# Output norm of a gated linear attention: one-column means, inverse roots on 16 columns, and transposes in place of wide products

## The reference, cut to what matters

```
o_g, s_new = gla(qg, kg, vg, la, s0)                       # (tokens, 4 heads, 256)
o_b = rmsnorm(o_g, g_gla_norm) * silu(gr)                  # mean over the 256 values of a head
merged = sigmoid(ga) * (o_a @ w_branch_a) + sigmoid(gb) * (o_b @ w_branch_b)
x = x + merged @ w_out                                     # then a mixture of 32 experts
```

## Time and profile before

| | |
|---|---|
| Median of 3 runs | 1103.74 us (1100.39 to 1105.07) |
| Span of the profiled execution | 1101.6 us; the profile gives no other time for it |
| PE busy | 1004.5 us (91% of the span) |
| DVE, ACT, POOL busy | 390.0, 281.0, 218.9 us |
| TensorE clock granted, mean of the span | 0.958 |
| Chain that ended last | PE 38%, transfers 26%, DVE 4% |

### The profile page before, as it was taken

The page is one execution under the profiler, slowest core; times in us unless marked ns, Lnnn a source line. Parts: engine busy times, 40 slices in busy tenths (PEclk is TensorE's granted clock), DMA queues, the critical chain, the costliest instruction groups (busy, mean ns, idle before and its releaser), DMA issues.

```text
span 1101.6 us, 15368 instructions
## 1 busy us (share of the span) xinstructions
PE 1004.5 (91%) x6369; PEld 696.1 (63%) x6369; DVE 390.0 (35%) x732; ACT 281.0 (26%) x456; POOL 218.9 (20%) x126
## 2 busy tenths in 40 slices
PE   8999999989999999999999899988787779877895
PEld 6996778869998799999997333333333433333232
DVE  7246333342786583322445211211101111111027
ACT  5435444455465452222215000000000000000012
POOL 0331121203221453443220011111001110011000
PEclk9999999999999999999999999988898899899898
DMA  9332512113211133343386999999999999999994
GB/s 232 79 90 77 180 41 58 39 39 96 58 41 49 48 97 86 116 130 96 124 364 245 373 424 427 425 425 426 429 427 427 428 426 429 429 426 425 423 412 152
DMA packets 108943, 267.57 MB, mean 243 GB/s; under 512 B 21821, under 2 KB 88797, under 8 KB 95666
## 3 DMA queue, kind: packets, MB, share of 16 engines
q1 hardware_dynamic: 104178, 258.06, 61.1%
q0 software_dynamic: 4704, 8.64, 2.1%
HBM read 256.12 MB, written 18.17 MB: 249 GB/s over the span
## 4 chain that ended last, share of the span: by engine, by line
PE 38%; DMA 26%; DVE 4%; issue 2%; ACT 1%; SPq 0%; DVEq 0%; POOLq 0%; ACTq 0%
DMA we<-in_w_exp_up 24%; PE proj L1062 18%; PE proj L1543 11%; PE proj L1559 3%; DMA zc<-expert_out 1%; PE bank L1389 1%; PE bank L1439 1%; DMA expert_out<-yo,sidx 1%; PE bank L1569 1%; PE proj L1345 1%; DVE x_rows L2637 1%; DVE xsT L2564 1%; ACT ex L1890 1%; PE proj L1545 0%; DVE x_rows L2644 0%
## 5 line engine op out<-in xcount | busy, mean ns | idle before, releaser
L1543 PE MATMUL proj<-we,xsT 128*64 128x512 f32 x512 | 249.1, 644 | 69.6 <-DMA we<-in_w_exp_up 61.5
L1545 PE MATMUL proj<-we,xsT 128*64 128x512 f32 x512 | 249.5, 644 | 0.0
L916 POOL TENSOR_TENSOR wlo<-raw,whi 128x1024 fp32r<-128x1024 f32 x68 | 156.2, 2298 | 382.1 <-PE proj L1062 358.9
L1543 PEld LDWEIGHTS proj<-we,xsT 128*64 128x64 f32 x512 | 73.2, 149 | 209.4 <-issue 193.4
L1062 PE MATMUL proj<-hT_hi,whi 128*128 128x272 f32 x688 | 146.4, 294 | 0.2 <-ACT grs L1824 0.2
L1062 PE MATMUL proj<-hT_hi,wlo 128*128 128x272 f32 x688 | 144.7, 292 | 0.0
L1062 PE MATMUL proj<-hT_lo,whi 128*128 128x272 f32 x688 | 144.5, 292 | 0.0
L2556 DVE TENSOR_TENSOR hg<-hg,proj 64x512 f32<-64x512 f32 x32 | 22.1, 690 | 309.1 <-ACT hg L2062 295.9
L2062 ACT ACTIVATE hg<-proj 64x512 f32<-64x512 f32 x30 | 17.7, 590 | 424.0 <-PE proj L1545 424.0
L1559 PE MATMUL proj<-we,hT 128*64 128x512 f32 x256 | 115.2, 592 | 2.0 <-DVE hT L2559 1.1
L1560 PE MATMUL proj<-we,hT 128*64 128x512 f32 x256 | 115.2, 593 | 0.0
(11 more groups left out here) (372 smaller groups left out, 1407.6 us busy)
## 6 DMA issues: line engine op xcount, KB each, us to landing
we<-in_w_exp_gate SPq DMA_DIRECT2D x31, 2048.0 KB, 32.1
we<-in_w_exp_up SPq DMA_DIRECT2D x31, 2048.0 KB, 36.5
we<-in_w_exp_down SPq DMA_DIRECT2D x31, 2048.0 KB, 38.8
raw<-in_w_in SPq DMA_DIRECT2D x43, 512.0 KB, 3.8
x_rows<-in_x_prompt SPq DMA_DIRECT2D x8, 512.0 KB, 4.8
raw<-in_w_branch_b SPq DMA_DIRECT2D x8, 512.0 KB, 3.9
raw<-in_w_out SPq DMA_DIRECT2D x8, 512.0 KB, 4.0
zc<-expert_out SPq DMA_DIRECT2D x4, 1024.0 KB, 17.6
```

Of the source, the lines that this page charges most:

```text
L916: nc.gpsimd.tensor_tensor(lo[:, 0:c], raw[n % NRAW][:, 0:c], hi[:, 0:c].bitcast(F32), ALU.subtract).then_inc(w_split, 1)
L1543: pe.matmul(proj[0:SLOTS, s, 0, :], xsT[:, k, cols], wg[:, k * FF:(k + 1) * FF], start=(k == 0), stop=(k == KD - 1))
L1545: mm = pe.matmul(proj[64:64 + SLOTS, s, 0, :], xsT[:, k, cols], wu[:, k * FF:(k + 1) * FF], start=(k == 0), stop=(k == KD - 1))
```

## The change

The means are no longer spread over 128 partitions by a wide product. DVE first adds the two squared tiles of a head (`sum_squares`). Then the squares are the stationary operand and one column of `mean256` moves through: each product gives the means of 128 tokens as one column, on the partitions of these tokens (`mean_columns`, two heads at a time, 16 products of one column for the four heads, each two matmul records). ACT takes the root of eight columns at once (`roots`), DVE inverts eight columns (`inverse_roots`), and PE turns each column back: it transposes the column, broadcast to 128x128, into a bank (`turn_roots`), so that the inverse roots stand on all 128 partitions. `normed_output` reads them there, in PSUM, instead of from SBUF. The decode tokens keep their wide form, with their bank changed.

PE's order changes too. `wa` 4 is issued in four parts, between which the decode outputs stand three, three and two, and the first turn of roots. The second one-column means stand behind `wa` 4. `ga` 5 is issued in eight parts, with the second turn of roots behind the second part and the decode means, head by head, behind parts 3 to 6.

```diff
@@ buffers
-    ors = [D_("ors0", [P, SEQ])]
...
-    ors.append(D_("ors1", [P, SEQ]))
+    o_root = D_("o_root", [P, 4 * GH])
@@ -722,6 +721,17 @@
     x_turned = bank[:, 0:2, :].rearrange("p a b -> p (a b)")[:, 0:TOK]
+    def root_col(h, i):
+        return 4 * h + i
+    def root_rows(h):
+        return bank[:, (1, 3)[h % 2], :]
+    COLUMNS_DONE, ROWS_DONE, DEC_DONE = (1, 4), (2, 3, 5, 6), 7
     def output_part(h):
         return (slice(None), slice(2 * h, 2 * h + 2), slice(0, SEQ)) if h < GH else (slice(None), slice(None), slice(SEQ, TOK))
@@ -1374,20 +1384,31 @@
             product("wa", c)
             new_values(c)
-        def o_mean(h):
-            pe.wait_ge(osq_ready, h + 1)
-            if h == 0:
+        def mean_columns(b):
+            pe.wait_ge(osq_summed, 2 * b + 2)
+            if b == 0:
                 pe.wait_ge(bS_ready, NT)
-            if h == 1:
-                pe.wait_ge(att_masked, NT)
-            if h == 2:
-                pe.wait_ge(kdT_copied, NT)
-            if h == 3:
-                pe.wait_ge(o_rms, 1)
-            for j in range(2):
-                mm = pe.matmul(bank[:, (0, 1, 3, 0)[h], :], mean256[:, :], osq[h % 2][:, j, :], start=(j == 0), stop=(j == 1))
+            for h in (2 * b, 2 * b + 1):
+                for i in range(4):
+                    at = root_col(h, i)
+                    mm = pe.matmul(bank[:, 0, at:at + 1], osq[h % 2][:, 0, i * P:(i + 1) * P], mean256[:, 0:1], start=True, stop=True)
             mm.then_inc(om_done, 1)
+        def turn_roots(b):
+            pe.wait_ge(o_rms, 2 * b + 2)
+            for h in (2 * b, 2 * b + 1):
+                if h == 0:
+                    pe.wait_ge(att_masked, NT)
+                if h == 1:
+                    pe.wait_ge(kdT_copied, NT)
+                if h >= 2:
+                    pe.wait_ge(og_ready, h - 1)
+                for i in range(4):
+                    at = root_col(h, i)
+                    mm = pe.transpose(root_rows(h)[:, i * P:(i + 1) * P], o_root[:, at:at + 1].to_broadcast([P, P]), ident)
+                mm.then_inc(om_done, 1)
         def last_outputs(n0, n1):
@@ -1399,23 +1420,34 @@
             return mm
-        o_mean(0)
+        mean_columns(0)
         new_values(NT - 1)
-        o_mean(1)
+        taken = take("wa", 4)
+        product_part("wa", 4, taken, 0, 4)
         pe.wait_ge(attT_copied, NT)
         pe.wait_ge(state_loaded, 16)
-        last_outputs(0, 4)
-        o_mean(2)
-        o_mean(3)
-        last_outputs(4, 8).then_inc(last_og, 1)
-        product("wa", 4)
-        pe.wait_ge(osq_ready, GH + 1)
-        pe.wait_ge(o_rms, 2)
-        for h in range(GH):
-            for j in range(2):
-                mm = pe.matmul(bank[:, 1, h * DEC:(h + 1) * DEC], mean256[:, :], osq_d[:, 2 * h + j, :], start=(j == 0), stop=(j == 1))
-        mm.then_inc(om_done, 1)
-        product("ga", 5)
+        last_outputs(0, 3)
+        turn_roots(0)
+        product_part("wa", 4, taken, 1, 4)
+        last_outputs(3, 6)
+        product_part("wa", 4, taken, 2, 4)
+        last_outputs(6, 8).then_inc(last_og, 1)
+        product_part("wa", 4, taken, 3, 4)
+        mean_columns(1)
+        taken = take("ga", 5)
+        for part in range(8):
+            product_part("ga", 5, taken, part, 8)
+            if part == 1:
+                turn_roots(1)
+            if part == 3:
+                pe.wait_ge(osq_ready, GH + 1)
+            if 3 <= part < 3 + GH:
+                h = part - 3
+                at = P + h * DEC
+                for j in range(2):
+                    mm = pe.matmul(bank[:, 0, at:at + DEC], mean256[:, :], osq_d[:, 2 * h + j, :], start=(j == 0), stop=(j == 1))
+                if h == GH - 1:
+                    mm.then_inc(om_done, 1)
         product("wa", 5)
         for j in range(EARLY_A):
             product("gb", j)
@@ -1930,7 +1962,7 @@
         def o_squares(h):
             if h >= 2:
-                act.wait_ge(om_done, h - 1)
+                act.wait_ge(om_done, COLUMNS_DONE[0])
             nc.scalar.activation(osq[h % 2][:, :, :], gqk[:, 2 * h:2 * h + 2, 0:SEQ], ACT.Square).then_inc(osq_ready, 1)
         for c in range(NT):
@@ -1959,41 +1991,38 @@
             act.sem_inc(proj_read[o % 2], 1)
             out_of("wa", c)
-        def o_root(h):
-            act.wait_ge(om_done, h + 1)
-            if h == 2:
-                act.wait_ge(og_ready, 1)
-            if h == 3:
-                act.wait_ge(og_ready, 2)
-            nc.scalar.activation(ors[h % 2][:, :], bank[:, (0, 1, 3, 0)[h], :], ACT.Sqrt, bias=eps_col[:, :]).then_inc(o_rms, 1)
+        def roots(b):
+            act.wait_ge(om_done, COLUMNS_DONE[b])
+            if b:
+                act.wait_ge(o_rms, 2)
+            cols = slice(8 * b, 8 * b + 8)
+            nc.scalar.activation(o_root[:, cols], bank[:, 0, cols], ACT.Sqrt, bias=eps_col[:, :]).then_inc(o_rms, 1)
         def o_high(h):
             act.wait_ge(og_ready, h + 1)
-            if 1 <= h <= 2:
-                act.wait_ge(om_done, h + 2)
+            if h == 1:
+                act.wait_ge(om_done, COLUMNS_DONE[1])
             part = output_part(h)
             nc.scalar.copy(ob_hi[part], gqk[part]).then_inc(ob_high, 1)
         act.wait_ge(proj_done, OUT_INDEX["ga", 4] + 1)
         next_high(WT_INDEX["ga", 4])
-        o_root(0)
+        roots(0)
         o_squares(2)
-        o_root(1)
         o_squares(3)
-        o_root(2)
         act.wait_ge(last_og, 1)
         step(nc.scalar.copy(gqk[:, :, SEQ:TOK], bank[:, 2, 0:2 * GH * DEC].rearrange("p (n l) -> p n l", l=DEC)))
         step.settle()
         nc.scalar.activation(osq_d[:, :, :], gqk[:, :, SEQ:TOK], ACT.Square).then_inc(osq_ready, 1)
+        roots(1)
         o_high(0)
-        o_root(3)
         chunk_gate(4)
         o_high(1)
         out_of("wa", 4)
         o_high(2)
-        act.wait_ge(om_done, GH + 1)
-        nc.scalar.activation(ors_d[:, :, :], bank[:, 1, 0:GH * DEC].rearrange("p (h l) -> p h l", l=DEC), ACT.Sqrt, bias=eps_col[:, :])\
+        act.wait_ge(om_done, DEC_DONE)
+        nc.scalar.activation(ors_d[:, :, :], bank[:, 0, P:P + GH * DEC].rearrange("p (h l) -> p h l", l=DEC), ACT.Sqrt, bias=eps_col[:, :])\
             .then_inc(o_rms, 1)
         gate_value(0, "ga", 5)
         o_high(3)
@@ -2358,6 +2387,11 @@
             o, ps = out_of("ga", c)
             v.tensor_copy(halves(gate_home(0, c)[:, :]), ps).then_inc(proj_read[o % 2], 1)
+        def sum_squares(h):
+            dve.wait_ge(osq_ready, h + 1)
+            v.tensor_tensor(osq[h % 2][:, 0, :], osq[h % 2][:, 0, :], osq[h % 2][:, 1, :], ALU.add).then_inc(osq_summed, 1)
         for c in range(NT):
             if c:
                 masked(c)
@@ -2370,25 +2404,35 @@
                 decayed(c + 1)
                 branch(0, c)
             else:
+                sum_squares(0)
+                sum_squares(1)
                 gate_out(4)
+        def inverse_roots(b):
+            dve.wait_ge(o_rms, 2 * b + 1)
+            cols = slice(8 * b, 8 * b + 8)
+            v.reciprocal(o_root[:, cols], o_root[:, cols]).then_inc(o_rms, 1)
         def normed_output(h):
-            dve.wait_ge(o_rms, h + 1)
-            inverse(ors[h % 2][:, :], ors[h % 2][:, :])
+            dve.wait_ge(om_done, ROWS_DONE[h])
             dve.wait_ge(og_gated, h + 1)
             og = gqk[:, 2 * h:2 * h + 2, 0:SEQ]
             for n in range(2):
-                last = v.scalar_tensor_tensor(og[:, n, :], og[:, n, :], g_gla[:, n:n + 1], ors[h % 2][:, :], ALU.mult, ALU.mult)
+                last = v.scalar_tensor_tensor(og[:, n, :], og[:, n, :], g_gla[:, n:n + 1], root_rows(h), ALU.mult, ALU.mult)
             last.then_inc(og_ready, 1)
+        inverse_roots(0)
+        sum_squares(2)
+        sum_squares(3)
         normed_output(0)
         normed_output(1)
-        normed_output(2)
         dve.wait_ge(last_og, 1)
         new_state(NT - 1)
+        inverse_roots(1)
         branch(0, 4)
+        normed_output(2)
         normed_output(3)
         dve.wait_ge(o_rms, GH + 1)
         inverse(ors_d[:, :, :], ors_d[:, :, :])
```

More of the change, by code:

```diff
@@ L562, in _build @@
     keys_ready = sem("keys_ready")
-    out_T = sem("out_T")
     out_copied = sem("out_copied")
@@ L594, in _build @@
     osq_ready = sem("osq_ready")
+    osq_summed = sem("osq_summed")
     om_done = sem("om_done")
@@ L1148, in _ @@
             pe.transpose(bank[:, 2, P + i * ROPE:P + (i + 1) * ROPE], kpeA[64:96, i * P:(i + 1) * P], ident[64:96, 64:96])
-        pe.transpose(bank[0:DEC, 2, 256:256 + ROPE], kpeA[64:96, SEQ + PAST:KEYS], ident[64:96, 64:96]).then_inc(out_T, 1)
+        pe.transpose(bank[0:DEC, 2, 256:256 + ROPE], kpeA[64:96, SEQ + PAST:KEYS], ident[64:96, 64:96]).then_inc(cache_T, 1)
         product("gr", 2)
@@ L2204, in _ @@
         v.tensor_copy(kpeA[64:96, SEQ:SEQ + PAST], bank[64:96, 0, 2 * P:4 * P]).then_inc(keys_ready, 1)
-        dve.wait_ge(out_T, 1)
+        dve.wait_ge(cache_T, 2)
```

## The result

The changed kernel takes 1109.67 us (median of 6 runs, 1106.85 to 1111.96), against 1100.95 us for the kernel before on the same chip: ratio 1.0058 [1.0039, 1.0077]. A second occasion gave 1108.59 against 1101.65, ratio 1.0059 [1.0036, 1.0082]. The ratios are not the quotients of the two medians (1.0079 and 1.0063); the text goes by the ratios, with their 95% intervals in brackets. Both intervals lie above 1, so the change makes the kernel slower, by about 0.6% or 6.5 us. The kernel before itself had medians from 1100.80 to 1103.74 us on different occasions. The profiled execution took 1109.11 us, with a span of 1106.9 us (1101.6 before).

The account below looks back on a forecast made before the run. PE was taken to bound the stretch up to `ga` 5, everything behind shifting alike. Terms at full clock gave -2.3 us, low clock +2.7, so +0.4 on 1103.74: 1104.1 us, range 1099.0 to 1109.0.

Parts of the forecast that it names:

- rival (2): Clock stays low from the first decode outputs through `ga` 5: +5.7 us, 1109.4 us; chance 0.09.
- the slowing thin records: One-column and decode records might double at low clock, at worst 5 us more; nothing was taken for it.
- The removed work: Wide means on PE's chain, 9.03 us; the 13.4 us that DVE loses were held worth nothing by themselves.
- Steps (a) to (c): Added on PE at full clock: one-column products 3.57 us, sixteen transposes 2.08, changes between products and other work 1.2.
- Step (d): New wait of PE ahead of `ga` 5 for low weights that POOL cuts behind the decode gating: 1.5 us.
- the term +2.7: Low-clock loss from about mid decode outputs into `ga` 5: 2.7 us, against 3.0 lost in the kernel before.
- the bound of 8: Upper bound on clock loss: all dense pieces from 381 us to the end of `ga` 5 low, 8 us more.
- fell to 0.5 after thin work each time: Reading of the earlier trace: granted clock 0.50 at 46 us after one-column products, and behind decode outputs at 384 and 390.
- Rival (1): Dense pieces between thin ones keep the clock up: -2.3 us, or -3.8 if `ga` 5's weights are early; chance 0.22.
- Rival (3): `wb` 0 becomes late as POOL and DVE slow each other: +0.4 plus 1 to 1.5 us, 1105.5 us; chance 0.07.
- Rival (4): Transposes do not keep the clock up, one more low spell: +1.6 us, so +2.0 and 1105.7 us; chance 0.04.
- The sign named in the prediction: `ga` 5 should end within 2 us of 402.7; an end after 406 would mean the clock was low for longer.

Follow-up runs that it names:

- parts_only: The changed kernel's order, with `wa` 4 and `ga` 5 in parts, but the old wide means; 1102.91 us, ratio 1.0018 against the kernel before.
- zero_narrow: Changed kernel with decode outputs' first product and state update over 128 rows, rows 32 to 127 zero, widths kept; 1100.78 us, ratio 0.9982 against the kernel before.
- zero_rows: Changed kernel with decode rows zero-filled to 128, and one-column products and decode outputs made 96 columns wide; 1098.48 us, ratio 0.9960 against the kernel before.
- parts_pool: parts_only with POOL cutting the low weights of `ga` 5 ahead of the decode gating; 1104.03 us, ratio 1.0020 against the kernel before.
- zero_before: Kernel before with decode outputs 96 columns wide, and their first product and the state update over 128 zero-filled rows; 1103.97 us, ratio 1.0016.
- after_again: The changed kernel, unaltered, measured and profiled a second time; 1108.59 us, ratio 1.0059 against the kernel before.
- spread_second: Changed kernel with second one-column products and second turn of roots inside `ga` 5, POOL cutting its weights before decode gating; 1111.01 us, ratio 1.0092 against kernel before.
- rows_full: Changed kernel with one-column products and decode outputs 96 columns wide, and 128 rows of chunk 3 replacing the decode tokens' 32; 1098.79 us, ratio 0.9974 against kernel before.
- before_wide: The kernel before with only the decode outputs widened from 32 to 96 columns; 1101.73 us, ratio 1.0005 against the kernel before.

## Why the prediction was right or wrong

The forecast was +0.4 us. The runs show about +6.5 us by the ratio, and the time of 1109.67 us lies above 1104.1 and 0.67 us above the range. What happened is rival (2), to which I gave 0.09, with the slowing thin records that it names as an addition. That its 1109.4 us is so near is luck: it was reached by 8 us lost on products, where the trace has 3.8 us lost on products and 5.6 elsewhere, and by adding a wait that did not occur. The pieces are start-to-start times summed over the stretch; "full clock" takes decode outputs from `parts_only` and the state update from before, the one-column products from `zero_narrow` (3.65), the rest from `zero_rows`.

| term | predicted | at full clock | in after |
| --- | --- | --- | --- |
| one-column products (32) | 3.57 | 3.65 | 5.15 |
| transposes (16) | 2.08 | 1.58 | 3.15 |
| `wa` 4 and `ga` 5, 9.11 without breaks | +0.8 to 1.6 | 9.94 (+0.83) | 13.73 |
| decode outputs (32 records) | unchanged | 5.09 | 6.92 |
| state update (8 records) | unchanged | 1.92 | 2.63 |
| wait at `ga` 5 | 1.5 | 1.6 (2.1 in `parts_only`) | 0 |

- **The removed work** was rightly read as 9.03 us on the chain and nothing for DVE by itself. `parts_pool` and `zero_before` add what the prediction missed: DVE's inversions cost nothing only as long as PE is slow.
- **Steps (a) to (c)** hold at full clock within 0.5 us each. They sum up, with the wait, to 0.22 + 3.65 + 1.58 + 9.94 + 5.09 + 1.92 + 1.45 (decode means) + 1.6 = 25.45 us, 3.4 less than the 28.88 before; -2.3 was forecast. The decode means are 0.25 us cheaper between parts of `ga` 5 (1.70 before), a term that the sum had as unchanged.
- **Step (d)**, the new wait, exists: 2.10, 1.59 and 1.62 us where PE runs at full clock (`parts_only`, `zero_rows`, `zero_narrow`), none in after, where PE's slower work hides it. That it was counted on top of a clock that is low ahead of it was an error of the sum. A low spell behind the wait is another matter: `zero_narrow` has both, 1.62 us of wait and then the low clock into `ga` 5.
- **The step that failed is the clock**, the term +2.7. By the table after pays (5.15 - 3.65) + (3.15 - 1.58) + (13.73 - 9.94) + (6.92 - 5.09) + (2.63 - 1.92) = 9.4 us for it, and saves the 1.6 of the wait: net 7.8. The 3.8 us on products were within the bound of 8, more than the 2.7 taken. Of the other 5.6 us, 3.3 (one-column products and decode outputs) come from the sentence "since they are far from limited by their columns I take nothing for it"; 2.3 (transposes and state update) had no price at the low clock at all. One-column and 32-column records do slow down at the low clock, 0.117 to 0.204 us and 0.33 to 0.56 us a pair, so that a time which hardly depends on the columns (0.117 us with one, 0.116 with 96) is no time that the clock leaves alone. Transposes too, 0.10 to 0.20. The earlier trace rows had shown 0.20 for 16 transposes ahead of the full clock; the price was in the rows and was not used.
- **The reading "fell to 0.5 after thin work each time"** holds for the trace of before and not for others. In `after_again` the same one-column products of the early norm run until 45.33 us and the granted clock is 1.00 in every stretch from 40 to 70 us. A fall at a hole isn't certain either: 2.10 us of wait at `ga` 5 in `parts_only` came with none, 2.09 us in `parts_pool` with 3.4 us of low clock.
- **Rival (1)**, that interleaving keeps the clock up, did not happen: with the thin arithmetic the dense parts did not hold the clock, and `spread_second` shows that more of it doesn't help. **Rival (3)**: no, `wb` 0 kept its cover of 1.1 us (416.27 against 417.35). **Rival (4)**, that transposes don't hold the clock up: in `zero_rows` it stays at 1.00 through both groups of eight, so they need not bring it down. No run took the transposes away, so their share in after stays open. The Trainium skill ("TensorE: Matmul & The Clock Gate", Part 4: PE-mode transpose) says that they don't count as activity; `zero_rows` gives no support to it, though eight are too few to refute it.
- The sign named in the prediction, `ga` 5 ending after 406, decided as said: the clock was low for longer.

What the runs show of the cause: 32 of 128 rows in 24 of the stretch's records (16 first products of decode outputs, 8 of the state update), together with the one-column ones, go with 20 us of low clock; filled rows with 6.8; filled rows and wider records with 3.4 (`rows_full`) or none (`zero_rows`). Before, wide means stood around the same decode records, and the low spells were short. Neither kind need bring it, as one profile each shows: the 32-row records were there in `parts_only` and `before_wide`, the products of the means, 96 columns wide, in `zero_rows`, all without a low spell. The decode outputs don't start it: in after and in `zero_narrow` the clock falls at about 378.3 us, behind the first one-column products and in the state update, and the first decode output begins at 381.5. What differs is how long it stays low. Why rows weigh more than width isn't settled: with filled rows the thin part is also shorter (3.4 us of decode records for 5.1), and no run tells these two apart.

## What to carry to other kernels

Price a replacement by small matrix records at both clock levels: a record whose time hardly depends on its columns slows down at the lower one like any other here, and a saving of 9 us in wide records can turn into a loss when what is left around it is thin. Look at the rows of neighbouring records too: padding a 32-row operand with zeros to 128 rows, for two memsets, turned this change from 0.6% slower to 0.2% faster than the kernel before, and to 0.4% faster with the records widened as well. A wait found by arithmetic at full clock must not be added to a slow clock ahead of it, since one hides the other. And where PE gets quicker, look at what it will then wait for: here DVE's inversions, free before, became the limit.

## What the runs showed of the hardware

- A gapless PE can lose its clock. In after, PE is busy for 2.00 of 2.00 us in every stretch from 378 to 402 us and the clock is 0.50 in most of them. The Trainium skill ("TensorE: Matmul & The Clock Gate", HAM oscillation — how this bites in real kernels) explains falls by idle gaps between bursts; that is `zero_before`'s case (a hole of 3.27 us, then 0.50), and not this one.
- Alternating records of 32 and of 128 rows cost 0.33 us a pair, records of 128 rows alone 0.22 (`zero_narrow`, 32 columns wide, full clock). The weight loads are the same length in the profile:

```profile
388.87 0.29 PEld L1418 LDWEIGHTS bank<-attT,vtok 32*128 32x128 f32 x2
389.20 0.30 PEld L1419 LDWEIGHTS bank<-exq,S_smp 128*128 128x128 f32 x2
```

  These are of after. Their starts are 0.33 us apart; the same two of `zero_narrow` start 0.22 apart:

```profile
384.55 0.30 PEld L1419 LDWEIGHTS bank<-exq,S_smp 128*128 128x128 f32 x2
384.77 0.30 PEld L1418 LDWEIGHTS bank<-attT,vtok 128*128 128x128 f32 x2
```

  The Trainium skill ("TensorE: Matmul & The Clock Gate", LDWEIGHTS (loading the stationary operand)) says that a 32x128 load takes as long as a 128x128 one. The durations agree; the starts are what differs. Both kinds of row, 32 and 128, begin later where they alternate, so I put the 0.11 us a pair down to the change between row counts. No run has 32-row decode records alone, so this is argued and not shown.
- One-column records of float32 cost 0.113 to 0.117 us at full clock, and the same records 96 columns wide 0.116 to 0.12 (1.86 us to the next start and 1.92 us of duration for 16 in `zero_rows`).
- DVE's multiplications of 128x512 take longer beside POOL when all their operands lie in SBUF: 2.91 us for two in `zero_before` against 1.42. With the inverse roots in PSUM, as the change has them, they don't, 0.68 us each beside POOL in `zero_rows`:

```profile
392.17 2.72 DVE L2426 SCALAR_TENSOR_TENSOR gqk<-gqk,gains,bank 128x512 f32<-128x512 f32 x4
390.81 4.76 POOL L934 TENSOR_TENSOR ob_lo<-gqk,ob_hi 128x1024 fp32r<-128x1024 f32 x2
```
